# Sample attention of a hybrid decoder step: products of two samples written as one product with a matrix of two blocks

## The reference, cut to what matters

```python
# latent (MLA) heads: a latent part of 128 channels and a rotated part of 32
s = (einsum('bthc,bsc->bhts', ql, ckv) + einsum('bthr,bsr->bhts', qr, kr)) * scale
p = softmax(where(causal, s, -inf))
# sparse (DSA) heads: an index score picks 256 keys of 2056, the others are masked
dots  = einsum('bthd,bsd->bths', iq, ik)                    # 64 channels
score = einsum('bth,bths->bts', iw, relu(dots))
_, idx = top_k(where(causal, score, -inf), 256)
p = softmax(where(valid, einsum('btgnd,btkgd->btgnk', q, k) * scale, -inf))
```

## Time and profile before

| | us |
|---|---|
| median of 3 runs | 2681.15 |
| lowest, highest | 2674.07, 2688.79 |
| the profiled execution | 2685.77 |
| span of its trace | 2684.1 |
| TensorE's matmuls busy in it | 2425.1 |
| VectorE busy in it | 1719.8 |
| mean granted TensorE clock | 0.884 |

### The profile page before, as it was taken

One profiled execution on the slowest core, in us unless ns is written; L12 is line 12 of the kernel. 1 busy time (PEld: TensorE's weight loads), 2 busy tenths in 40 slices (PEclk: granted clock), 3 DMA queues, 4 the chain that ended last, 5 costly groups with the idle time before them and its releaser, 6 DMA issues. The chain is left out here.

```text
span 2684.1 us, 38680 instructions
## 1 busy us (share of the span) xinstructions
PE 2425.1 (90%) x13219; PEld 1926.4 (72%) x13219; DVE 1719.8 (64%) x3536; ACT 895.7 (33%) x1419; POOL 816.7 (30%) x847
## 2 busy tenths in 40 slices
PE   6978998888768989797999999799999999999997
PEld 3533454366546445596999999788888888888886
DVE  2235873466620113487999996367888787778786
ACT  2012233111112012332566665333344334334333
POOL 0001013430100000230000001277777788774221
PEclk9985789655578985898999999899999999999998
DMA  4000002323223300222677777758999898999994
GB/s 178 10 6 16 1 16 72 107 81 92 88 67 126 141 8 1 68 69 73 192 246 242 237 244 267 240 176 289 350 363 347 305 326 316 314 315 322 312 320 148
DMA packets 215805, 475.74 MB, mean 177 GB/s; under 512 B 30561, under 2 KB 123106, under 8 KB 213730
## 3 DMA queue, kind: packets, MB, share of 16 engines
q1 hardware_dynamic: 156354, 304.12, 34.0%
q0 software_dynamic: 54688, 165.59, 17.0%
q10 hardware_dynamic: 4608, 4.20, 0.5%
HBM read 432.07 MB, written 41.74 MB: 177 GB/s over the span
## 5 line engine op out<-in xcount | busy, mean ns | idle before, releaser
L1992 PE MATMUL psC<-xh,Uh 128*128 128x256 f32 (+1 forms) x2048 | 615.8, 301 | 45.0 <-DVE Ul L1855 43.6
L1992 PE MATMUL psC<-xh,Ul 128*128 128x256 f32 (+1 forms) x2048 | 607.7, 297 | 0.0
L1992 PE MATMUL psC<-xl,Uh 128*128 128x256 f32 (+1 forms) x2048 | 607.1, 296 | 0.0
L1992 PEld LDWEIGHTS psC<-xh,Uh 128*128 128x128 f32 x2048 | 389.2, 190 | 60.0 <-DVE Ul L1855 29.8
L1992 PEld LDWEIGHTS psC<-xh,Ul 128*128 128x128 f32 x2048 | 389.2, 190 | 5.0
L1992 PEld LDWEIGHTS psC<-xl,Uh 128*128 128x128 f32 x2048 | 389.2, 190 | 0.0
L1760 POOL DMA_INDIRECT ring<-in_peer_v,idxV x256 | 304.3, 1189 | 255.2 <-DVE h L1901 165.3
L1855 DVE TENSOR_TENSOR Ul<-rU,Uh 128x1024 fp32r<-128x1024 f32 x256 | 311.7, 1218 | 75.7 <-ACT Uh L1796 75.3
L1768 POOL DMA_INDIRECT aS<-acts,idxA x256 | 318.0, 1242 | 127.2 <-issue 77.8
L1901 DVE SCALAR_TENSOR_TENSOR h<-ring,wS,h 128x1024 f32<-128x1024 f32 x256 | 328.0, 1285 | 17.5 <-DMA ring<-in_peer_v,idxV 16.5
L1796 ACT ACTIVATE Uh<-rU 128x1024 fp32r<-128x1024 f32 x256 | 270.2, 1056 | 153.8 <-DMA rU<-in_peer_uT 149.4
(11 more groups left out here) (269 smaller groups left out, 3810.3 us busy)
## 6 DMA issues: line engine op xcount, KB each, us to landing
rU<-in_peer_uT SPq DMA_DIRECT2D x256, 512.0 KB, 4.1
rV<-in_peer_v SPq DMA_DIRECT2D x128, 512.0 KB, 4.5
gates<-gst POOLq DMA_DIRECT2D x10, 2048.0 KB, 10.0
gr<-gates SPq DMA_DIRECT2D x32, 640.0 KB, 7.6
arena<-in_poolM SPq DMA_DIRECT2D x128, 128.0 KB, 2.0
acts<-stage SPq DMA_DIRECT2D x32, 512.0 KB, 4.9
wraw<-in_w_pq SPq DMA_DIRECT2D x16, 512.0 KB, 3.5
arena<-in_w_in SPq DMA_DIRECT2D x8, 884.0 KB, 16.2
```

The lines of the kernel that those rows point to most:

```text
L1992: last = M(bank(6 + k, hi - lo), a[:, at, c], x[:, d, lo:hi], start=(d == 0 and a is Uh and x is xh), stop=(d == KD - 1 and x is xl))
```

## The change

Three kinds of products of two samples become one each, with a matrix that holds the queries of one sample in one block of rows and columns, those of the other in another, and zeros elsewhere.

- *Index scores:* iqTs gets each sample's queries on its own 64 partitions and zeros on the other 64; one product of 128 channels by 128 query rows takes the place of two.
- *Rotated parts:* qrTs grows from 2 x 64 to 4 x 128 columns; sample b has its queries on partitions 32 (b % 4), in columns 64 (b % 2) of its pair's block. krT is loaded to partitions 32 (b % 4) accordingly. One product over 64 (even pairs) or 128 partitions (odd pairs, and the new keys) by 128 query rows takes the place of two.
- *Masks:* the causal one of the new keys and the one of the DSA pairs are added for 128 query rows at once.

For this the loops of pair_scores are turned about: chunks outside, samples inside, and the joint product behind the page products of both. The zeros are set by two further POOL instructions at the start; VectorE copies the index queries in 2 instructions of half the size and the rotated queries in 8 of half the size (4 before).

```diff
@@ the tile and its zeros
-        qrTs = sb("qrTs", [P, 2, 64])
+        qrTs = sb("qrTs", [P, NB // 2, P])
             pool.memset(bdq[:], 0.0).then_inc(S["c16"], 1)
+            pool.memset(qrTs[:], 0.0).then_inc(S["c16"], 1)
+            pool.memset(iqTs, 0.0).then_inc(S["c16"], 1)
@@ loads of krT (POOL)
-                    load_page(pool, krT[32 * p:32 * p + 32, b2, j * PAGE:(j + 1) * PAGE], "krT", b, j, kr_in[p])
+                    g = 32 * (b % 4)
+                    load_page(pool, krT[g:g + 32, b // 4, j * PAGE:(j + 1) * PAGE], "krT", b, j, kr_in[p])
@@ copies of the index queries of the samples (VectorE); its and TensorE's other waits on c16 go from 4 to 6 too
+                    dve.wait_ge(S["c16"], 6)
                     for j in range(2):
-                        last = V.tensor_copy(iqTs[64 * j:64 * j + 64].rearrange("p b h t -> p h b t"),
-                                             bank(7, p1=64).rearrange("p (h b t) -> p h b t", h=8, b=NB))
+                        own = "p (q j h t) -> p j h q t"
+                        last = V.tensor_copy(
+                            iqTs[64 * j:64 * j + 64].rearrange("p b h t -> p (b h t)")
+                            .rearrange(own, j=2, h=8, t=NQ)[:, j],
+                            bank(7, p1=64).rearrange("p (h q j t) -> p j h q t", h=8, j=2, t=NQ)[:, j])
@@ copies of the rotated queries (VectorE)
-                    for p in range(NB // 2):
-                        last = V.tensor_copy(qrTs[32 * p:32 * p + 32].rearrange("p b (h t) -> p h b t", h=8),
-                                             bank(7, p1=32).rearrange("p (h b t) -> p h b t", h=8, b=NB)
-                                             [:, :, 2 * p:2 * p + 2, :])
+                    for b in range(NB):
+                        g, c = 32 * (b % 4), 64 * (b % 2)
+                        last = V.tensor_copy(qrTs[g:g + 32, b // 2, c:c + 64].rearrange("p (h t) -> p h t", h=8),
+                                             bank(7, p1=32).rearrange("p (h b t) -> p h b t", h=8, b=NB)[:, :, b, :])
@@ index scores (TensorE)
-                for b2 in range(2):
-                    H = slice(64 * b2, 64 * b2 + 64)
-                    q = iqTs[H, 2 * p + b2, :, :].rearrange("p h t -> p (h t)")
-                    k = ikT[H, p, kc * 512:kc * 512 + 512] if kc < 4 else kT[H, 3, SEQ:NTOK]
-                    last = M(bank(5 + i % 2, n, p0=64 * b2, p1=64 * b2 + 64), q, k, start=True, stop=True)
-                last.then_inc(S["xi_mm"], 1)
+                q = iqTs[:, 2 * p:2 * p + 2, :, :].rearrange("p b h t -> p (b h t)")
+                k = ikT[:, p, kc * 512:kc * 512 + 512] if kc < 4 else kT[:, 3, SEQ:NTOK]
+                M(bank(5 + i % 2, n), q, k, start=True, stop=True).then_inc(S["xi_mm"], 1)
@@ pair_scores (TensorE)
-                for b2 in range(2):
-                    b = 2 * p + b2
-                    for kc in range(5):
...
-                            last = M(out, qrTs[G, b2, :], k, start=False, stop=(kc < 4), skip_group_check=True)
...
-                            last = M(out, same16[:, b, :], mbs[:, kc * 512:kc * 512 + n], start=False, stop=True,
-                                     skip_group_check=True)
+                for kc in range(5):
+                    n = 512 if kc < 4 else NS
+                    for b2 in range(2):
+                        b = 2 * p + b2
...
+                        for a in range(4 if kc < 4 else 1):
...
+                            o = bank(kc, k.shape[-1], a * PAGE, p0=64 * b2, p1=64 * b2 + 64)
+                            M(o, q, k, start=(a == 0), stop=False, skip_group_check=True)
+                    if kind == 0:
+                        G = slice(0, 64 if p % 2 == 0 and kc < 4 else P)
+                        k = krT[G, p // 2, kc * 512:kc * 512 + 512] if kc < 4 else kT[:, 1, SEQ:NTOK]
+                        last = M(bank(kc, n), qrTs[G, p, :], k, start=False, stop=(kc < 4), skip_group_check=True)
+                        if kc == 4:
+                            last = M(bank(kc, n), same[:, 128 * p:128 * p + 128], cst[0:NS, C_NEW:C_NEW + NS],
+                                     start=False, stop=True, skip_group_check=True)
+                    else:
+                        last = M(bank(kc, n), same16[:, 2 * p:2 * p + 2, :].rearrange("p b c -> p (b c)"),
+                                 mbs[:, kc * 512:kc * 512 + n], start=False, stop=True, skip_group_check=True)
```

More of the change, by code:

```diff
@@ L577, in _ @@
                 else:
+                    dve.wait_ge(S["c16"], 6)
                     for j in range(2):
-                        last = V.tensor_copy(iqTs[64 * j:64 * j + 64].rearrange("p b h t -> p h b t"),
-                                             bank(7, p1=64).rearrange("p (h b t) -> p h b t", h=8, b=NB))
+                        own = "p (q j h t) -> p j h q t"
[3 more added lines that the diff above has]
+                            bank(7, p1=64).rearrange("p (h q j t) -> p j h q t", h=8, j=2, t=NQ)[:, j])
                     last.then_inc(S["tB_ev"], 1)
             dve.wait_ge(S["tA_ev"], 2 * NBLK)
-            dve.wait_ge(S["c16"], 4)
+            dve.wait_ge(S["c16"], 6)
             for g in range(2):
@@ L1027, in _ @@
             pe.wait_ge(S["vm_ev"], 4)
-            pe.wait_ge(S["c16"], 4)
+            pe.wait_ge(S["c16"], 6)
             pe.wait_ge(S["ix_relu"], 24)
@@ L1083, in pair_scores @@
                     pe.wait_ge(S["mbs_done"], 1)
-                for b2 in range(2):
-                    b = 2 * p + b2
-                    for kc in range(5):
-                        n = 512 if kc < 4 else NS
-                        out = bank(kc, n, p0=64 * b2, p1=64 * b2 + 64)
-                        if kind == 0:
[L1090 to L1099, removed]
-                            last = M(out, qrTs[G, b2, :], k, start=False, stop=(kc < 4), skip_group_check=True)
-                            if kc == 4:
-                                last = M(out, same[:, 64 * b:64 * b + 64], cst[0:NS, C_NEW:C_NEW + NS],
-                                         start=False, stop=True, skip_group_check=True)
@@ L1104, in pair_scores @@
+                for kc in range(5):
+                    n = 512 if kc < 4 else NS
+                    for b2 in range(2):
+                        b = 2 * p + b2
+                        if kind == 0:
+                            q = qlTs[:, b, :, :].rearrange("p h t -> p (h t)")
                         else:
                             q = bdq[:, b, :, :, :].rearrange("p g n t -> p (g n t)")
[L1106 to L1112, removed]
@@ L1113, in pair_scores @@
-                            last = M(out, same16[:, b, :], mbs[:, kc * 512:kc * 512 + n], start=False, stop=True,
-                                     skip_group_check=True)
+                        for a in range(4 if kc < 4 else 1):
+                            if kc < 4:
+                                k = KV[:, slot, b2, 4 * kc + a, 0:128]
+                            else:
+                                k = kT[:, (0, 2)[kind], SEQ:NTOK]
+                            o = bank(kc, k.shape[-1], a * PAGE, p0=64 * b2, p1=64 * b2 + 64)
+                            M(o, q, k, start=(a == 0), stop=False, skip_group_check=True)
```

## The result

The changed kernel takes 2583.1 us (median of 4 runs, 2578.5 to 2588.2), the one before 2679.8 in the same comparison: a ratio of 0.9631, with a 95% interval of 0.9600 to 0.9662. The profiled execution has a span of 2586.5 us, 97.6 less.

The account below looks back on a forecast made before the run. TensorE was taken to bound the MLA pairs, with VectorE next. The terms -76.8 (MLA) - 23.3 (DSA) + 1.0 (index) + 0.6 (setup) = -98.5 us took 2685.8 to 2587.3, or 2583 by the median; stated range 2568 to 2616.

Parts of the forecast that it names:

- The bound: Sample attention: TensorE sets the 61.1 us MLA period; VectorE, free 16.6 us before its end, comes next.
- MLA scores: Scores of an MLA pair fall from 32.7 to 10.9 us; VectorE's waits limit the saving to 76.8 us in all.
- I take full overlap: MLA page products on two column halves run together: both samples' pages take 1.90 us per chunk at the low clock.
- The reading of L975: Sixteen instructions on four column quarters take 1.09 us at the high clock, so all quarters ran side by side.
- rival 1: Column halves do not overlap: MLA saves 69 us, DSA 7; 2607 us, chance 0.19; with low clock too 2643, 0.04.
- VectorE's limit: VectorE's waits ahead of the MLA row maxima cap the MLA saving at 76.8 us; beyond that VectorE takes over.
- The rule on program order: Skill rule that matmuls start and end strictly in program order; the second half's first could overlap only the first half's last.
- The clock: In MLA scores the clock rises from low to high after 4.5 us, making a pair 10.9 us.
- Rival 2: Halves overlap, but the MLA scores stay at clock 0.50: 87 us saved, 2594 us; chance 0.10.
- DSA: DSA scores of a pair take 7.5 to 8.0 us, 5.8 us less, four times: 23.3 us saved.
- Index and setup: Joint index products win nothing, weight loads cost 1 us; eight rotated-query copies cost 0.6 us, shorter index copies 0.

Follow-up runs that it names:

- turned_by_page: Kernel before with turned loops, page products alternating between the two samples page by page, rotated products or masks side by side, nothing joint; ratio 0.9633.
- again: The changed kernel once more, unedited, as the base of its group of runs; ratio 0.9666 to the kernel before.
- joint_only: Changed kernel with all page products of one sample, then all of the other, then the joint products; ratio 0.9653, 2590.0 us.
- turned_only: Kernel before with turned loops: per chunk one sample's pages, the other's, then two rotated products or masks side by side, nothing joint; ratio 0.9637.

## Why the prediction was right

The time came out as forecast, 2583, and the mechanism was right in the main: TensorE's scores bounded MLA, the products of two samples now share their time, and VectorE's idle time capped the gain. That the number hit to the us is luck: the sum behind it was too large in two terms, and time won in stages that no edit was aimed at covered that.

- *The bound.* Right: MLA was TensorE's, VectorE came next, and it now limits two of the four maxima and the mask; the third is still TensorE's, and at the fourth both end together (a wait of 0.26 us).
- *MLA scores.* 76.8 us were forecast, 70.8 measured between the sums' copy and the fourth maximum (218.7 us before, 147.8 after). The step that failed is "I take full overlap": the pages cost 2.81 and 1.51 us, not 1.90 and 1.02. The reading of L975 was true but had four instructions a quarter; with eight, the case rival 1 named as not in any row, the overlap is half. A block took 11.2 to 15.4 us instead of 10.9, and VectorE's limit hid most of it.
- *The rule on program order.* The prediction names it from the Trainium skill (TensorE: Matmul & The Clock Gate, Part 3): matmuls start and end in program order. By it the two halves of eight would take 15 steps of 16, four and four 13, two and two 9; they took about 12, 8 and 8, and a second half's first matmul started ahead of the first half's sixth. The measurement decides against it as a rule for separate column halves.
- *The clock.* A rise in every MLA block, as assumed, though after some 3 to 9 us where it began low (the mean clocks of 0.71 to 0.90 give 2.5 to 8.9), not 4.5; the first began high, which I had not thought of. Rival 2, the low clock all through, is what turned_by_page does. What makes the clock rise in one order and not in another stays open.
- *DSA.* 23.3 us forecast, 16.4 measured (171.9 to 155.4 us from the fourth MLA maximum to the end): blocks of 9.0 to 10.1 us, not 7.5 to 8, for the same half overlap. Waits for pages moved along as said.
- *Index and setup.* +1.0 forecast, +1.1 measured; the eight copies +0.6 as forecast (1.17 to 1.81 us); the index copies took 0.5 less (1.38 to 0.85 us), which I had put at 0. Whether either reached the index scores the runs do not show, as the clock moves the stage between by more.
- *What made up for it.* The changes add up to 86 us between the two profiles, not 98.5. Of the other 12, 9 lie ahead of the index scores, where only these copies and the two POOL fills changed, and 3 behind the sample stage (1806.5 to 1803.7 us; all runs lie from 1801.6 to 1808.2). By averages over the profiles the sample stage is 89.5 us shorter (five profiles with the old pairs average 392.7, two of the changed kernel 303.2), the copy of the sums comes some 4 earlier (five with the old index copies average 483.7, eight with the new 480.0), and some 1 us is won behind (1805.8 with the old pairs, 1804.4 in the nine others): 94 to 95 us, where the medians differ by 96.7 in the first group and by 95.0 in that of *again*. The 4 are less than the 12 us by which that place moves in one kernel; whether they belong to the change stays open.
- *The reason for the gain.* I had it in the overlap of pages and in the joint product. The runs show that neither is needed for it. Before, the products of the two samples ran one sample behind the other, at the low clock; standing together, two rotated products cost one, joint or not. For the pages either the overlap (turned_by_page, 16.4 us at the low clock) or the rise of the clock (joint_only, 13.8 us without overlap) was enough, since VectorE's limit hides what lies below.

## What to carry to other kernels

Before two small products are merged with a matrix of zeros, put them next to each other on different parts of the array: here that alone gave all of the gain (ratio 0.9637 against 0.9631 and 0.9666 with the matrix). Read the next engine's idle time ahead of the one that bounds a stage; it caps the gain in that stage (76.8 us here, of which 70.8 were reached), and it made six different orders of TensorE's work equally fast. A forecast that lands on the time should still be taken apart by stages: two terms were too large by 6 and 7 us, and stages that no edit was aimed at covered it.

## What the runs showed of the hardware

- Products on different column halves overlap by how they are dealt out: two and two instructions or four and four overlap fully (1.02 and 1.08 us for sixteen at the high clock), eight and eight half (1.51). The second half's first matmul started with the first half's fifth, at both clocks.
- Two 32 x 64 products on the same rows and different columns, four instructions, take 1.01 us at the high clock and 1.90 at the low one, where one alone took 1.89.
- The granted clock went with the order of the same products, in one profile each: alternating by page (turned_by_page), four blocks of 16.4 to 16.6 us ran at 0.50 to their ends; with eight and eight (turned_only), every block rose to the high level (means of 0.86 and 0.87).
- The time of a stage that no edit touched moved by 12 us between profiles of the same kernel (475.1 to 487.1), with the granted clock of 222 to 300 us (0.81 and 0.63).
